# Pooling and gated delta layers: joint products of 512 columns, pooling sums by shifted additions, four PSUM banks a block

## Chip, cores and metric

The kernel runs on one core of one Trainium2 chip. The metric is the device time of one execution in microseconds (us); lower is better.

## What is computed

Two blocks of a network over 256 tokens of 2048 channels, all in float32, one after the other: a retention layer, a pooling layer, and then a block of several branches, one of them a gated delta rule. The change touches the pooling layer and the projections and the convolution of the delta rule:

```python
# pooling layer: h is the normalized input, windows 2, 4, 8, 16, one per group of 1024 channels
p = h @ w_in;  u, z = jnp.split(p, [POOL_WIDTH], axis=-1)      # 4096 channels each
win_sum = cs[:, 1:, gi] - jnp.take(cs[:, :, gi], lo, axis=1)   # cs: running sum of u over the tokens
pooled.append(win_sum / cnt)                                   # cnt = min(t + 1, w)
...
mix = (pooled - uf)
mix = jnp.einsum('bsgc,gcd->bsgd', mix, w_grp) + b_grp
return (mix.reshape(B, S, POOL_WIDTH) * scale * silu(z)) @ w_out

# delta branch: q, k, v of 2048 channels each, 16 heads of 128, z_a their output gate
qkv, z_a, ... = jnp.split(rmsnorm(x, g_pre) @ w_in, ...)
qkv = silu(causal_depthwise_conv(qkv, w_conv_qkv))             # 4 taps along the tokens
q, k, v = jnp.split(qkv, 3, axis=-1);  q, k = l2norm(q), l2norm(k)
A = einsum('bhnid,bhnjd->bhnij', k * beta, k) * decay * strict # strictly lower triangular
T = triangular_solve(eye + A, eye)
u, w = T @ (v * beta), T @ (k * beta * exp(gc))                # then a scan over chunks of 64 tokens
o_a = rmsnorm(scan(...)) * silu(z_a);  y_a = o_a @ w_br_a
```

## The kernel before

**The weight stream.** All weights come as 900 chunks of 512 KB, each two k-tiles of 128 rows by 512 columns, through a ring of four slots. For each chunk, SP issues the load into `raw` (once VectorE has split the slot's last one: semaphore `lo_done`), ScalarE rounds it to `whi` (`split_hi`, L626, once TensorE has finished the slot's last products: semaphore `multiplied`), VectorE subtracts for the rest, `wlo` (`split_lo`, L1078), and TensorE multiplies. The activations stand likewise split, as `aH` and `aL`, turned so that channels lie on the partitions. A product in full precision is the sum of three: high by high, high by low, low by high. Each engine's program is written out in order, so a helper that waits holds all behind it on that engine. A step `j` below is the chunk that TensorE is at; the splits of that step are of chunk `j + 4`.

**Two forms of a chunk.** `chunk_a` (L1930 to L1932) takes the activations as the stationary operand and gives tokens on the partitions: 12 products 512 wide. `chunk_b` (L1955, L1957, L1958) takes the weights as the stationary operand and gives channels on the partitions, 24 products 256 wide:

```python
mm(half(bank, c), whi[:, s, k, w], aH[:, kt + k], ...)
mm(half(bank, c), whi[:, s, k, w], aL[:, kt + k], ...)
ins = mm(half(bank, c), wlo[:, s, k, w], aH[:, kt + k], ...)
```

**Pooling stage** (from about 792 us, `group` on PE, ACT and DVE). Four groups, one per window, of 40 chunks: two blocks of 8 chunks give `u`, two give `z`, and 8 more chunks are the group's product with `w_grp`. All are `chunk_a`. `u` is scaled by its rows' root mean square, split into `pUH` and `pUL`, and at step 19 TensorE multiplies it with a 0/1 matrix (`pMH`) less the window's size on the diagonal: 32 products of 256 or 128 columns into banks 4 to 7. ScalarE and VectorE split those into `mH` and `mL` (L640 onwards), the stationary operand of the last 8 chunks.

**Delta stage** (from 1367 us, `delta` and `delta_late`). Four groups of four heads and 32 chunks: blocks k, q and v in `chunk_b`, with two PSUM banks each (0 and 1, 2 and 3, by turns), and the gate z in `chunk_a`. After each of the first three, ScalarE writes the convolution's last tap from PSUM (`conv_first`) and VectorE adds the other three taps from PSUM, one per step (`conv`, L1497, semaphore `conv_tap`). In step 13 VectorE forms `aT`, the eight matrices A of the group (L1574). The inverse of its 32 x 32 diagonal blocks is GpSimd's (`inverse`, 62 operations): SP takes the blocks out by DMA at step 15 (`diag_in`), back at step 16, and after the inverse out and in again at LV - 5 and LV - 4 (`diag_out`, to `iU`). LV is 34, so such steps fall into the next group's steps 0 and later. VectorE turns `iU` to `iT` (L1429, step LV - 2) and from step LV on TensorE fills in the blocks below the diagonal (`below`, first product on `iT` at L2112) and runs the scan, with VectorE's and ScalarE's steps of `delta_late` in between, down to the product of `oD` with the gate at LV + 12 (L1467) and its turning at LV + 16 to LV + 20. So between steps 13 and 34 VectorE has splits, the convolution's taps, `oD` of the group before, decays and turnings in one queue, ahead of `iT`.

Of the kernel before, what the change touches and what calls it, by code (L numbers as in the profile page):

```python
# [11 lines left out]

# [4 lines left out]
F32 = mybir.dt.float32  # L17
# [64 lines left out]
WARM = 16  # L82
NORM1_AT = {0: 2, 1: 3, 4: 4, 5: 5, 6: 6, 7: 7}
# [18 lines left out]
C_END = C_WIN + GROUPS * NT  # L102
# [7 lines left out]
def build(nc, dram):  # L110
    with ExitStack() as outer:
# [19 lines left out]
        aH = sb(outer, "aH", [P, 16, SEQ], F32R)  # L131
        aL = sb(outer, "aL", [P, 16, SEQ], F32R)
# [17 lines left out]
        with ExitStack() as s:  # L150
# [20 lines left out]
            with ExitStack() as r:  # L171
# [3 lines left out]
                pUH = sb(r, "pUH", [P, NT, GDIM], F32R)  # L175
                pUL = sb(r, "pUL", [P, NT, GDIM], F32R)
# [5 lines left out]
                pM = sb(r, "pM", [P, 3 * P])  # L182
                pMH = sb(r, "pMH", [P, 3 * P], F32R)
# [7 lines left out]
        with ExitStack() as s:  # L191
            oaH = sb(s, "oaH", [P, 16, SEQ], F32R)
            oaL = sb(s, "oaL", [P, 16, SEQ], F32R)
            with ExitStack() as r:
# [50 lines left out]
                eE = sb(r, "eE", [P, E_REAL, NT, NB])  # L245
# [35 lines left out]

        cum_rows = nc.dram_tensor("cum_rows", [NT, DN_HEADS, P], F32).ap()
# [27 lines left out]
        pu_sb, pu_lo, pz_sb, mix_ps, mix_hi, mix_lo, pm_in, pb_in, mz_add, mz_sb, pb_used = (  # L310
            sem(n) for n in "pu_sb pu_lo pz_sb mix_ps mix_hi mix_lo pm_in pb_in mz_add mz_sb pb_used".split())
# [6 lines left out]
            sem(n) for n in "dn_in conv0_sb conv_tap kqv_sb dt_sub dt_sb sq_sb sqn_sb en_sb gk_sb".split())  # L318
        scratch_out, dt_in, xn_in, u_in = (sem(n) for n in "scratch_out dt_in xn_in u_in".split())
# [44 lines left out]
        def half(bank, c):  # L364

            return PS[:, bank + c // 2, (c % 2) * SEQ:(c % 2 + 1) * SEQ]

# [21 lines left out]
        def _(sp):  # L389
# [54 lines left out]
            def delta_dma(i, first):  # L444
                q = i * (D_PER // RING) + (D_AT // RING + 2)
                for j in range(D_PER):
# [11 lines left out]
                    if j == 15:  # L458
# [5 lines left out]
                    if j == 16:  # L464
# [4 lines left out]
                    if j == LV - 5:  # L469
# [4 lines left out]
                    if j == LV - 4:  # L474
# [26 lines left out]
        def _(pool):  # L501
# [19 lines left out]
            pool.dma_start(pM[:], dram["pm"][0]).then_inc(pm_in, 16)  # L521
            row_scale(M_N2)

            def bias(i):

                pool.wait_ge(mix_hi, i * 4 + 4)
# [3 lines left out]
            with pool.Fori(1, P_N) as i:  # L530

                pool.wait_ge(pb_used, i)
                pool.dma_start(pM[:], dram["pm"][i]).then_inc(pm_in, 16)
# [47 lines left out]
            pool.wait_ge(const_set, 3)  # L581
# [37 lines left out]
        def _(act):  # L619
# [107 lines left out]
            def group(i, first):  # L727
                q = i * (P_PER // RING) + P_AT // RING
                for j in range(P_PER):
                    split_hi(q, j + RING)  # L730
                    if first and j == 1:
                        t_split_hi(T_N2 + 3, aH, 12, lambda c: C_PN + 12 + c)
                    if not first and j in (8, 16):
                        group_tail(i - 1, j // 8 - 1)
                    if j in (7, 15):
                        done(act, q, j)
                        b = j // 8
                        act.wait_ge(row_rstd, M_N2 + 1)
# [1749 lines left out]
```

## Time and profile before

| what | us |
|---|---|
| three runs: lowest, median, highest | 2625.94, 2626.36, 2626.94 |
| span of the profiled execution | 2624.1 |
| pooling stage, one group, as in the profile's windows | 112.53 |
| delta stage, one group | 108.20 |

The profiled execution is one of its own; its span runs from its first instruction to its last. The median of the three runs lies 2.3 us above that span, which is what lies around it. The windows of the profile give the busy time of each engine in a stretch; the timeline gives each instruction's start and length in us with, in brackets, how long its engine had been idle before it and what ended that idle time. Lengths of products on TensorE overlap, so only the distance of their starts, or the time of a whole chunk, is a price.

### The profile page before, as it was taken

The numbers are of one execution on the slowest core, as the hardware profiler recorded it, in microseconds if no ns is written. First come the engines' busy times: TensorE is split into PE (matmuls) and PEld (weight loads), VectorE is DVE, ScalarE is ACT, GpSimd is POOL, SyncE is SP. The second block draws the span as 40 slices with busy tenths as digits, with TensorE's granted clock in tenths as the row PEclk, the third lists the DMA queues.
The fourth block names the chain that finished last, engine by engine and source line by source line (L and its number), as shares of the span: only waits on it lengthen the run. The fifth ranks groups of instructions, "written<-read, shape, count | busy, mean of one in ns | idle before, by whom it ended". The sixth has DMA issues, their size and how long they took to land.

```text
span 2624.1 us, 36684 instructions
## 1 busy us (share of the span) xinstructions
PE 2608.1 (99%) x13284; PEld 2218.9 (85%) x13284; DVE 1960.0 (75%) x2764; ACT 1321.0 (50%) x1683; POOL 168.0 (6%) x329
## 2 busy tenths in 40 slices
PE   9999999999999999999999999999999999999998
PEld 7888888888888888888889999998888888788887
DVE  5888877776755766757457786977798999989565
ACT  5444444444444544444456454454666666564453
POOL 0000000000000000000000341413000000000000
PEclk9999999999999999999999999999999999999999
DMA  8555555555655555556655555655555655655754
GB/s 309 179 187 177 179 185 185 184 191 190 198 193 192 195 196 192 196 185 217 196 189 176 173 165 159 194 159 175 176 197 191 197 192 187 200 188 194 247 175 159
DMA packets 151674, 499.69 MB, mean 190 GB/s; under 512 B 28736, under 2 KB 29472, under 8 KB 151008
## 3 DMA queue, kind: packets, MB, share of 16 engines
q1 hardware_dynamic: 148736, 486.18, 56.0%
q0 software_dynamic: 2784, 11.40, 1.4%
q8 instruction: 104, 1.70, 0.3%
q14 instruction: 50, 0.41, 0.0%
HBM read 493.30 MB, written 4.21 MB: 190 GB/s over the span
## 4 chain that ended last, share of the span: by engine, by line
PE 97%; DVE 2%; ACT 1%; issue 0%; DMA 0%; POOL 0%; SPq 0%; DVEq 0%; ACTq 0%
PE PS L1930 27%; PE PS L1932 27%; PE PS L1931 27%; PE PS L1955 4%; PE PS L1957 4%; PE PS L1958 4%; PE PS L2096 2%; DVE yl L1624 1%; DVE wlo L1078 0%; PE PS L2103 0%; PE PS L1966 0%; PE PS L2112 0%; DVE yl L1615 0%; PE PS L2010 0%; PE PS L2020 0%
## 5 line engine op out<-in xcount | busy, mean ns | idle before, releaser
L1078 DVE TENSOR_TENSOR wlo<-raw,whi 128x1024 fp32r<-128x1024 f32 x899 | 1096.9, 1225 | 595.8 <-ACT whi L626 591.1
L626 ACT CAST whi<-raw 128x1024 fp32r<-128x1024 f32 x899 | 939.6, 1049 | 1180.7 <-PE PS L1932 1009.4
L1930 PE MATMUL PS<-whi,aH 128*128 128x512 f32 x2160 | 844.1, 391 | 3.2 <-DVE wlo L1137 1.9
L1931 PE MATMUL PS<-wlo,aH 128*128 128x512 f32 x2160 | 840.6, 389 | 0.0
L1932 PE MATMUL PS<-whi,aL 128*128 128x512 f32 x2160 | 840.6, 389 | 0.0
L1930 PEld LDWEIGHTS PS<-whi,aH 128*128 128x128 f32 x2160 | 405.6, 188 | 88.1 <-issue 2.3
L1932 PEld LDWEIGHTS PS<-whi,aL 128*128 128x128 f32 x2160 | 405.5, 188 | 84.6
L1931 PEld LDWEIGHTS PS<-wlo,aH 128*128 128x128 f32 x2160 | 405.6, 188 | 82.9
L1955 PE MATMUL PS<-aH,whi 128*128 128x256 f32 x768 | 220.8, 288 | 1.5 <-DVE aL L1114 1.5
L1957 PE MATMUL PS<-aL,whi 128*128 128x256 f32 x768 | 217.1, 283 | 0.0
L1958 PE MATMUL PS<-aH,wlo 128*128 128x256 f32 x768 | 217.1, 283 | 0.0
L1932 PE MATMUL PS<-whi,oL 128*128 128x512 f32 x512 | 199.2, 389 | 0.0
L1930 PE MATMUL PS<-whi,oH 128*128 128x512 f32 x512 | 199.2, 389 | 0.0
L1931 PE MATMUL PS<-wlo,oH 128*128 128x512 f32 x512 | 199.2, 389 | 0.0
L1955 PEld LDWEIGHTS PS<-aH,whi 128*128 128x128 f32 x768 | 147.0, 191 | 2.5 <-issue 1.7
L1957 PEld LDWEIGHTS PS<-aL,whi 128*128 128x128 f32 x768 | 147.2, 192 | 0.1
L1958 PEld LDWEIGHTS PS<-aH,wlo 128*128 128x128 f32 x768 | 147.0, 191 | 0.0
L1624 DVE SCALAR_TENSOR_TENSOR yl<-up,wl,yl 128x256 f32<-128x256 f32 x272 | 113.3, 478 | 0.2
L1931 PEld LDWEIGHTS PS<-wlo,oH 128*128 128x128 f32 x512 | 96.1, 188 | 20.1
L1932 PEld LDWEIGHTS PS<-whi,oL 128*128 128x128 f32 x512 | 96.1, 188 | 20.1
L1930 PEld LDWEIGHTS PS<-whi,oH 128*128 128x128 f32 x512 | 96.1, 188 | 19.6
L1930 PE MATMUL PS<-whi,oaH 128*128 128x512 f32 x256 | 99.9, 390 | 0.0
(357 smaller groups left out, 2570.6 us busy)
## 6 DMA issues: line engine op xcount, KB each, us to landing
raw<-in_stream SPq DMA_DIRECT2D x900, 512.0 KB, 3.3
xT<-in_xT SPq DMA_DIRECT2D x4, 512.0 KB, 7.6
H<-in_x SPq DMA_DIRECT2D x4, 512.0 KB, 10.0
pB<-in_pool_b POOLq DMA_DIRECT2D x4, 512.0 KB, 4.5
iT<-diag_in SPq DMA_DIRECT2D x16, 128.0 KB, 3.7
bg<-in_b_gate POOLq DMA_DIRECT2D x8, 256.0 KB, 3.8
out<-eb SPq DMA_DIRECT2D x8, 256.0 KB, 2.2
dmask<-in_dmask SPq DMA_DIRECT2D x4, 384.0 KB, 5.8
```

The costliest lines, as they stand in the source:

```text
L626: nc.scalar.copy(whi[:, s], raw[:, s]).then_inc(hi_done, 1 + blank)
L1078: nc.vector.tensor_tensor(wlo[:, s], raw[:, s], whi[:, s].bitcast(F32), ALU.subtract).then_inc(lo_done, 1 + blank)
L1624: nc.vector.scalar_tensor_tensor(out=to, in0=up[:, c, k:k + SEQ], scalar=w, in1=yl[:, c], op0=ALU.mult, op1=ALU.add).then_inc(long_tap[c], 1)
L1930: mm(out, hi[:, kt + k, tok], whi[:, s, k], start=kt + k == 0, stop=False)
L1931: mm(out, hi[:, kt + k, tok], wlo[:, s, k], start=False, stop=False)
L1932: ins = mm(out, lo[:, kt + k, tok], whi[:, s, k], start=False, stop=last and k == KPC - 1)
L1955: mm(half(bank, c), whi[:, s, k, w], aH[:, kt + k], start=kt + k == 0 and c % 2 == 0, stop=False, skip_group_check=True)
L1957: mm(half(bank, c), whi[:, s, k, w], aL[:, kt + k], start=False, stop=False, skip_group_check=True)
L1958: ins = mm(half(bank, c), wlo[:, s, k, w], aH[:, kt + k], start=False, stop=end, skip_group_check=True)
L2096: ins = mm(PS[rows, bank + n, h * P + at:h * P + at + width], lhsT(t, h), rhs(t, h), start=h == 0, stop=True, skip_group_check=True)
```

## The change

**Wide products.** `aH` and `aL` now lie side by side in one array `aHL`, so one product takes both: 512 columns, of which the low half of the result (high by high) lies in the first 256 columns of a PSUM bank and the other (high by low) in the last 256. The product with `wlo` is added to the first half, 256 wide. So a chunk of this form has 8 products 512 wide and 8 products 256 wide, and each 128 channels take a whole bank, four banks a block. The two halves are added later: ScalarE copies one from PSUM, and VectorE adds the other from PSUM. In the delta stage blocks k, q and v all use banks 0 to 3 and z 4 and 5; the new `chunk_b` waits per bank until it is emptied, and orders its first and last chunk by banks. The convolution reads the sum, `xc`, from SBUF.

**Pooling.** The two `u` blocks have the new form (`chunk_w`), so `u` now stands with channels on the partitions and tokens along the row. The products with the 0/1 matrix go; VectorE scales (`rrow`, a row of factors that GpSimd's queue brings through a DRAM array), adds `u` to itself shifted by 1, 2, 4 and 8 as the window needs (`window_sum`, with zeros in a margin of `PAD` columns), and combines with the window's size, in the steps of `SUM_AT`. Banks change places, and so do TensorE's waits.

**Order in the delta stage.** The splits around the last chunk of a block stand behind the additions, the `oD` product two and its last turn two steps later, `ke` two steps later, the decays at step 10. SP takes the diagonal blocks out at steps 13 and 14, not 15 and 16, and the inverse at LV - 6 and LV - 5.

```diff
+ADD_AT = (9, 17)
+SUM_AT = ((11, 13, 15, 18, 19, 20), (21, 23, 24, 25, 26, 27))
+SPLIT_AT = (22, 29)
+EVICT_AT = tuple(b * K16 + K16 - 1 for b in range(3))
...
-        aH = sb(outer, "aH", [P, 16, SEQ], F32R)
-        aL = sb(outer, "aL", [P, 16, SEQ], F32R)
+        aHL = sb(outer, "aHL", [P, 16, 2, SEQ], F32R)
+        aH, aL = aHL[:, :, 0], aHL[:, :, 1]
...
@@ SP, delta stage
-                    if j == 15:
+                    if j == 13:
                         sp.wait_ge(a_sb, i + 1)
...
-                    if j == 16:
+                    if j == 14:
                         sp.wait_ge(scratch_out, i * 128 + 80)
...
-                    if j == LV - 5:
+                    if j == LV - 6:
                         sp.wait_ge(inv_done, i + 1)
...
-                    if j == LV - 4:
+                    if j == LV - 5:
...
@@ ScalarE, group and delta
+                        nc.scalar.copy(pU[:, b, :, PAD:], wide(b)[:, :, SEQ:]).then_inc(pu_lo, 1)
...
+            def low_half(i, y, q, j):
+                n = 3 * i + y
...
+                for c in range(HG):
+                    if c < HG - 1:
+                        act.wait_ge(qkv_ps, n * 3 + c + 1)
+                    else:
+                        done(act, q, j)
+                    nc.scalar.copy(xc[:, c], PS[:, c, SEQ:]).then_inc(conv0_sb, 1)
...
+                    if j in EVICT_AT:
+                        low_half(i, EVICT_AT.index(j), q, j)
                     split_hi(q, j + RING)
...
-                    if j == (11 if first else 8):
+                    if j == 11:
                         act.wait_ge(dt_sub, i + 1)
...
@@ VectorE, group
+                        if j == ADD_AT[b]:
+                            dve.wait_ge(pu_lo, i * 2 + (b + 1))
+                            u = pU[:, b, :, PAD:]
+                            nc.vector.tensor_tensor(u, wide(b)[:, :, 0:SEQ], u, ALU.add).then_inc(pu_sb, 1)
+                        if j in SUM_AT[b][:i + 3]:
+                            window_sum(i, b, SUM_AT[b].index(j))
...
@@ VectorE, delta
-                if n == LV + 12:
+                if n == (LV + 14 if i < D_N - 1 else LV + 12):
                     dve.wait_ge(ors_sb, i + 1)
...
-                if i < D_N - 1 and n in (LV + 16, LV + 17, LV + 18, LV + 20):
+                if i < D_N - 1 and n in (LV + 16, LV + 17, LV + 18, LV + 22):
...
+            def both_halves(i, y):
+                for c in range(HG):
+                    dve.wait_ge(conv0_sb, (3 * i + y) * 8 + c + 1)
+                    nc.vector.tensor_tensor(xc[:, c], PS[:, c, 0:SEQ], xc[:, c], ALU.add).then_inc(conv_tap, 1)
...
-                    split_lo(q, j + RING)
+                    if j in EVICT_AT:
+                        both_halves(i, EVICT_AT.index(j))
+                        split_lo(q, j - 1 + RING)
+                    if j + 1 not in EVICT_AT:
+                        split_lo(q, j + RING)
...
-                    if j == 14:
+                    if j == 16:
                         dve.wait_ge(ke_sb, i * 2 + 1)
...
@@ TensorE
+            def chunk_b(q, j, kt, n, last):
...
+                by_column = last or kt == 0
+                for a, b in product(range(QT if by_column else KPC), range(KPC if by_column else QT)):
+                    c, k = (a, b) if by_column else (b, a)
+                    if kt + k == 0 and n is not None:
+                        pe.wait_ge(conv_tap, (n - 1) * 16 + c + 1)
+                    w = slice(c * P, (c + 1) * P)
+                    mm(PS[:, c], whi[:, s, k, w], aHL[:, kt + k].rearrange("p a n -> p (a n)"), start=kt + k == 0, stop=False,
+                       skip_group_check=True)
+                    ins = mm(PS[:, c, 0:SEQ], wlo[:, s, k, w], aH[:, kt + k], start=False, stop=last and k == KPC - 1,
+                             skip_group_check=True)
+                    if last and k == KPC - 1 and c < QT - 1:
+                        ins.then_inc(qkv_ps, 1)
...
-                pe.wait_ge(mix_lo, i * 4 + 4)
                 for w in range(2):
-                    pe.wait_ge(pz_sb, i * 2 + (w + 1))
                     for k in range(4):
+                        if not w and k % 2 == 0:
+                            pe.wait_ge(mix_lo, i * 2 + (k // 2 + 1))
```

Two places in the engines' order follow, each before and after. A row is a line, an operation, its result and operands, its size, and in brackets the semaphores that it waits for. The first is VectorE in the delta stage, group 1, from step 13 on. `raw` to `wlo` is a chunk's split, `aT` are the matrices A, `oD` the product with the gate for group 0, `ke` the scaled keys, `yD` the convolution's taps. Before:

```order
L1078 TENSOR_TENSOR wlo<-raw,whi 128x1024 [waits hi_done]
L1570 TENSOR_TENSOR ed<-en,dT 128x4 [waits en_sb,dt_sb]
L1574 SCALAR_TENSOR_TENSOR aT<-PS,en,dT 128x128 [waits a_ps]
L1574 SCALAR_TENSOR_TENSOR aT<-PS,en,dT 128x128 x7
L1078 TENSOR_TENSOR wlo<-raw,whi 128x1024 [waits hi_done]
L1467 SCALAR_TENSOR_TENSOR oD<-oD,oms,zD 128x128 [waits zd_sb,ors_sb]
L1467 SCALAR_TENSOR_TENSOR oD<-oD,oms,zD 128x128 x7
L1581 TENSOR_SCALAR ke<-PS,ed 128x128 [waits ke_sb]
L1581 TENSOR_SCALAR ke<-PS,ed 128x128 x3
L1078 TENSOR_TENSOR wlo<-raw,whi 128x1024 [waits hi_done]
L1497 SCALAR_TENSOR_TENSOR yD<-PS,wcv,yD 128x255 [waits conv0_sb,multiplied]
L1497 SCALAR_TENSOR_TENSOR yD<-PS,wcv,yD 128x255 [waits conv0_sb] x3
```

After:

```order
L1123 TENSOR_TENSOR wlo<-raw,whi 128x1024 [waits hi_done]
L1643 TENSOR_TENSOR ed<-en,dT 128x4 [waits en_sb,dt_sb]
L1647 SCALAR_TENSOR_TENSOR aT<-PS,en,dT 128x128 [waits a_ps]
L1647 SCALAR_TENSOR_TENSOR aT<-PS,en,dT 128x128 x7
L1572 TENSOR_TENSOR xc<-PS,xc 128x256 [waits conv0_sb] x4
L1123 TENSOR_TENSOR wlo<-raw,whi 128x1024 [waits hi_done] x2
L1565 SCALAR_TENSOR_TENSOR yD<-xc,wcv,yD 128x255 [waits conv0_sb] x4
L1123 TENSOR_TENSOR wlo<-raw,whi 128x1024 [waits hi_done]
L1535 SCALAR_TENSOR_TENSOR oD<-oD,oms,zD 128x128 [waits zd_sb,ors_sb]
L1535 SCALAR_TENSOR_TENSOR oD<-oD,oms,zD 128x128 x7
L1654 TENSOR_SCALAR ke<-PS,ed 128x128 [waits ke_sb]
L1654 TENSOR_SCALAR ke<-PS,ed 128x128 x3
```

The four additions to `xc` now stand right behind `aT`, ahead of two splits that stood before and after the `oD` product; `oD` and `ke` come behind them.

The second is TensorE at the change from block q to block v (the second to the third) in the same group, the last products of one chunk and the first of the next. Before:

```order
L1958 MATMUL PS<-aH,wlo 128x256
L1955 MATMUL PS<-aH,whi 128x256 [waits lo_done,conv_tap]
L1957 MATMUL PS<-aL,whi 128x256
L1958 MATMUL PS<-aH,wlo 128x256
L1955 MATMUL PS<-aH,whi 128x256
```

After:

```order
L2032 MATMUL PS<-aHL,wlo 128x256
L2030 MATMUL PS<-aHL,whi 128x512 [waits conv_tap,lo_done]
L2032 MATMUL PS<-aHL,wlo 128x256
L2030 MATMUL PS<-aHL,whi 128x512
L2032 MATMUL PS<-aHL,wlo 128x256
L2030 MATMUL PS<-aHL,whi 128x512 [waits conv_tap]
L2032 MATMUL PS<-aHL,wlo 128x256
```

Before, the first product waits for a bank emptied a block earlier; now each bank's first product waits for the additions on the block just finished.

## Rows read from the trace of the kernel before

**Rows 1.** Page: span, busy engines, chain that ended last.

```profile
span 2624.1 us, 36684 instructions
...
PE 2608.1 (99%) x13284; PEld 2218.9 (85%) x13284; DVE 1960.0 (75%) x2764; ACT 1321.0 (50%) x1683; POOL 168.0 (6%) x329
...
PE 97%; DVE 2%; ACT 1%; issue 0%; DMA 0%; POOL 0%; SPq 0%; DVEq 0%; ACTq 0%
```

**Rows 2.** Windows: length, busy PE, PEld, DVE, ACT, POOL, clock; pooling, delta, within delta.

```profile
1017.61:1130.14 112.53, 112.53 (x514) 93.83 (x513) 75.92 (x95) 52.44 (x61) 1.07 (x2) 1.00 0.59 194
1482.30:1590.50 108.20, 108.20 (x884) 103.69 (x884) 87.02 (x165) 55.08 (x70) 33.95 (x66) 1.00 0.54 168
...
1531.40:1588.50 57.10, 57.10 (x395) 53.34 (x393) 55.55 (x107) 28.97 (x36) 29.77 (x63) 1.00 0.60 184
```

**Rows 3.** Timeline of ACT: start, length; splits in pooling, then in delta.

```profile
1083.06 1.05 ACT L626 CAST whi<-raw 128x1024 fp32r<-128x1024 f32 x1 [1.67 <-PE PS L1932]
1085.78 1.05 ACT L626 CAST whi<-raw 128x1024 fp32r<-128x1024 f32 x1 [1.67 <-PE PS L1932]
...
1534.45 1.05 ACT L626 CAST whi<-raw 128x1024 fp32r<-128x1024 f32 x1 [1.83 <-PE PS L1958]
1537.33 1.05 ACT L626 CAST whi<-raw 128x1024 fp32r<-128x1024 f32 x1 [0.36 <-PE PS L1958]
```

**Rows 4.** Timeline of TensorE, delta stage: start, length, two neighbouring products.

```profile
1531.31 0.28 PE L1955 MATMUL PS<-aH,whi 128*128 128x256 f32 x1
1531.43 0.28 PE L1957 MATMUL PS<-aL,whi 128*128 128x256 f32 x1
```

**Rows 5.** Chain: start, length; first products that read `iT`, groups 0 to 3.

```profile
1482.30 1.02 PE PS L2112 x32
...
1590.46 1.02 PE PS L2112 x32
...
1698.61 1.02 PE PS L2112 x32
...
1806.29 1.08 PE PS L2112 x32
```

**Rows 6.** Timeline of DVE: `iT` of group 0, stretch of group 1, `iT` again.

```profile
1479.68 1.25 DVE L1429 STREAM_TRANSPOSE iT<-iU 128x1024 f32<-128x1024 f32 x1 [0.73 <-DMA iU<-diag_out]
...
1530.99 2.15 DVE L1574 SCALAR_TENSOR_TENSOR aT<-PS,en,dT 128x128 f32<-128x128 f32 x8
1533.06 1.22 DVE L1078 TENSOR_TENSOR wlo<-raw,whi 128x1024 fp32r<-128x1024 f32 x1
...
1586.42 1.23 DVE L1078 TENSOR_TENSOR wlo<-raw,whi 128x1024 fp32r<-128x1024 f32 x1
1588.51 1.25 DVE L1429 STREAM_TRANSPOSE iT<-iU 128x1024 f32<-128x1024 f32 x1 [0.86 <-DMA iU<-diag_out]
...
1697.04 1.25 DVE L1429 STREAM_TRANSPOSE iT<-iU 128x1024 f32<-128x1024 f32 x1 [0.97 <-DMA iU<-diag_out]
...
1804.98 1.25 DVE L1429 STREAM_TRANSPOSE iT<-iU 128x1024 f32<-128x1024 f32 x1 [0.75 <-DMA iU<-diag_out]
```

**Rows 7.** Groups by shape: busy, mean ns; four subtractions on the timeline.

```profile
L640 ACT CAST aH<-PS 128x256 fp32r<-128x256 f32 x16 | 4.8, 387 | 5.4 <-PE PS L1966 5.4
L1401 DVE TENSOR_TENSOR sg<-PS,bg 128x1024 f32<-128x1024 f32 x8 | 9.8, 1221 | 0.1
...
2440.98 1.41 DVE L1112 TENSOR_TENSOR oaL<-PS,oaH 128x256 fp32r<-128x256 f32 x4
```

**Rows 8.** Timeline of DVE in the pooling stage, one split.

```profile
1056.94 1.23 DVE L1078 TENSOR_TENSOR wlo<-raw,whi 128x1024 fp32r<-128x1024 f32 x1 [1.49 <-ACT whi L626]
```

**Rows 9.** Timeline of the DMA queue SP, delta group 1.

```profile
1539.14 1.85 SPq L462 DMA_DIRECT2D diag_in<-aT  x4
...
1581.14 2.55 SPq L473 DMA_DIRECT2D diag_out<-xi  x4
```

**Rows 10.** Timeline of DVE while GpSimd inverts, delta group 3.

```profile
1778.19 1.38 DVE L1078 TENSOR_TENSOR wlo<-raw,whi 128x1024 fp32r<-128x1024 f32 x1
```

More of the change, by code:

```diff
@@ L11 @@
 from contextlib import ExitStack
+from itertools import product
 import concourse.bass as bass
@@ L366, in half, with wide, steps_before @@
             return PS[:, bank + c // 2, (c % 2) * SEQ:(c % 2 + 1) * SEQ]
+        def wide(b):
+            return PS[:, 4 - 4 * b:8 - 4 * b]
+        def steps_before(i, b):
+            return sum(2 * (g + 5) for g in range(i)) + b * (i + 5)
         def heads(bank):
@@ L751, in group @@
                         b = j // 8 - 2
[L752 removed]
+                        if first and b == 0:
+                            act.wait_ge(row_rstd, M_N2 + 1)
+                        by_token(pZ[:, :, b * NB:(b + 1) * NB], 4 + 2 * b, ACT.Silu, M_N2, pz_sb)
             def group_tail(i, w):
@@ L1545, in delta @@
                         delta_late(i - 1, j + D_PER)
[L1546 removed]
+                    if first and j == 7:
+                        bias_decays()
+                        for k in range(1, TAPS):
+                            conv(i, 0, k)
+                        decays()
+                    if not first and 7 <= j <= 9:
+                        conv(i, 0, j - 6)
+                    if not first and j == 10:
                         dve.wait_ge(dt_in, i * (16 * NT))
                         log_decays(i, dT)
[L1549 to L1560 removed]
                     if first and j == 14:
@@ L1952, in chunk_b @@
                     for c in range(QT):
-                        w = slice(c * P, (c + 1) * P)
-                        end = last and k == KPC - 1
-                        mm(half(bank, c), whi[:, s, k, w], aH[:, kt + k], start=kt + k == 0 and c % 2 == 0, stop=False,
+                        w, out = slice(c * P, (c + 1) * P), wide(b)[:, c]
+                        mm(out, whi[:, s, k, w], aHL[:, kt + k].rearrange("p a n -> p (a n)"), start=kt + k == 0, stop=False,
                            skip_group_check=True)
-                        mm(half(bank, c), whi[:, s, k, w], aL[:, kt + k], start=False, stop=False, skip_group_check=True)
-                        ins = mm(half(bank, c), wlo[:, s, k, w], aH[:, kt + k], start=False, stop=end,
+                        ins = mm(out[:, 0:SEQ], wlo[:, s, k, w], aH[:, kt + k], start=False, stop=last and k == KPC - 1,
                                  skip_group_check=True)
@@ L2163, in delta @@
                     b = j // K16
-                    if j == 0 and not first:
-                        pe.wait_ge(conv_tap, i * 36)
-                    if j == K16 and not first:
-                        pe.wait_ge(zd_sb, i)
-                    if j == 2 * K16 or j == 3 * K16:
-                        pe.wait_ge(conv_tap, i * 36 + 12 * (b - 1))
+                    if j == 3 * K16:
+                        pe.wait_ge(sq_sb, i * 2 + 2)
+                    if first and j == 1:
+                        pe.wait_ge(ee_sb, 2)
                     if first and j in (1, 3, 5):
```

209 lines of the change are left out of this document (114 added, 95 removed).

## The prediction

> **What bounds the kernel now.** I read the page first: TensorE is busy for 99% of 2624.1 us and carries 97% of the chain that ended last [rows 1]. So a shorter TensorE stream pays in full, as long as no other engine becomes late. Next the windows: a pooling group takes 112.53 us and a delta group 108.20, TensorE busy throughout at the full 2.4 GHz (granted clock 1.00), VectorE 75.92 and 87.02 [rows 2]. These averages mislead: inside a delta group, from 1531.4 to 1588.5, VectorE is busy 55.55 of 57.10 us [rows 2]. Its timeline there is one unbroken queue from the split at 1533.06, right behind the `aT` operations, to the split at 1586.42 (19 splits with other work between them), then 0.86 us of waiting for a DMA, then the transpose of `iT` [rows 6]. TensorE's first product on `iT` follows: at 1482.30, 1590.46, 1698.61 and 1806.29 for the four groups [rows 5], against `iT` done at 1480.93, 1589.76, 1698.29 and 1806.23 (start plus 1.25) [rows 6]. The margin is 1.37, 0.70, 0.32 and 0.06 us. So TensorE sets the pace in both stages, and in the delta stage VectorE is just in time, three groups out of four.
>
> The price of a product comes from the splits that TensorE releases: one per chunk, 2.72 us apart in pooling and 2.88 in delta [rows 3]. 12 products of 512 columns in 2.72 us is 0.2267 each; 24 products of 256 in 2.88 is 0.1200, as the starts 1531.31 and 1531.43 show [rows 4]. The lengths in the timeline (0.28) overlap and are no price. At 2.4 GHz the columns alone take 0.2133 and 0.1067, so each product has a fixed 13.3 ns, whatever its width.
>
> **Part 1, wide products in delta.** Per pair of k-tile and 128-column block, three 256-column products become one of 512 and one of 256. A chunk of 8 pairs costs 8 x (0.2267 + 0.1200) = 2.773 us against 2.88, 0.107 less. Three blocks of 8 chunks in 4 groups: 96 x 0.107 = **-10.2 us**, all on TensorE's path. The alternation of widths is not in the trace; its bounds are 0 (a wide product as dear as two narrow ones) and twice the 13.3 ns, from which I take the fixed part as the two neighbouring widths give it. The Trainium skill ("TensorE: Matmul & The Clock Gate", Back-to-back issue gap) gives about 2.5 ns beside the columns; by it 768 pairs would save 1.9 us. The rows here show five times that, at two widths alike, so the trace does not agree with it.
>
> **Part 2, pooling.** The sums on TensorE go: 112.53 - 40 x 2.72 = 3.73 us per group, -14.9 in all. Two of the four projection blocks change from 12 products of 512 to 8 of 512 and 8 of 256: 2.773 against 2.72, 16 chunks a group, 64 x 0.053 = +3.4. Together **-11.5 us**. VectorE takes the sums over: per half group an addition from PSUM, a scaling, one to four shifted additions, a last combination, each 1024 wide, 1.22 us by the nearest row [rows 7]. They stand one to a step from step 17 to 29, each beside a split: 1.23 [rows 8] + 1.22 = 2.45 us of a 2.72 us chunk; today the queue idles 1.49 us per step there [rows 8]. TensorE reads the result at chunks 32 and 34, and the last split of it stands at step 29, so I cost it at nothing; the four-dimensional operands have no row, and at twice the price the longest group would fall behind 0.9 us a step over 12 steps, 10 us, of which some 5 is covered by the ring of four chunks: +5 at most. ScalarE has fewer operations than now.
>
> **Part 3, four banks a block.** With 512 columns per 128 channels a block fills banks 0 to 3, so the next block must wait until its bank is emptied: ScalarE copies the low half (0.387 us, nearest row) and VectorE adds the other half (0.42) [rows 7]. This happens 8 times with TensorE waiting (blocks 0 to 1 and 1 to 2), the third block's successor uses banks 4 and 5. Take block 1 to 2 of group 1. Chunk 15 begins at 1531.31 and by the new column order finishes a bank every 0.693 us. ScalarE learns of a finished chunk 0.26 us late (1531.31 + 2.88 = 1534.19, and its split starts at 1534.45 [rows 3]). It is held by a 1.05 us split to 1532.6, and copies the banks then and at 1533.0, 1533.65 and 1534.34. VectorE comes free from `aT` at 1533.06, so bank 0 is added by 1533.5; chunk 16 wants it at 1534.08, and each further bank 0.693 later, which the additions keep ahead of (the last at 1535.2 against 1536.2). TensorE waits for none: cost 0, upper bound 0.6 us each, 5 in all, if VectorE were a microsecond later.
>
> **Part 4, what these additions do to VectorE's queue.** Here I expect the gain of Part 1 to go. All of it stands in the saturated stretch. The four additions of step 15 finish at 1535.2 instead of releasing VectorE at 1533.06: 2.1 us, mostly waiting for TensorE's last column, with the splits of chunks 18 and 19 queued behind. The four at step 23 find their data ready: 1.41 us [rows 7]. The rest of the queue is the same work in another order (the `od` product and the last turn of `oD` a few steps later, the decay logarithms from step 6 to 10, where there was idle time). So `iT` is 3.5 us later in VectorE's own time, less the DMA wait, which goes. TensorE comes sooner: 12 chunks x 0.107 = 1.28 us (9 chunks in the last group, 0.96). Wait before the first product on `iT`: group 1, 3.5 + 1.28 - 0.70 - 0.86 = 3.2; group 2, 3.5 + 1.28 - 0.32 - 0.97 = 3.5; group 3, 3.5 + 0.96 - 0.06 - 0.75 = 3.65. Group 0 has no tail of an earlier group in its queue and idles in between; its 1.37 + 0.73 is enough, 0. Sum **+10.4 us**. A split that is late earlier in the stretch makes TensorE wait there and by as much less at `iT`.
>
> **Part 5, the transfers sooner.** On SP the four reads of `aT` issue at 1539.14 today, though `aT` is ready at 1533.1 [rows 6, 9]; two steps earlier they start about 6 us sooner, and GpSimd's inverse with them. Behind them SP holds the loads of chunks 22 and 23 for some 3 us. A load goes out when a slot's split is done and has some four chunks, 11 us, until the next split of that slot must be; I cost 3 us of that at nothing, and at 3 us a group if VectorE's lag had used it up. At the other end the write at 1581.14 [rows 9] moves a step up, but behind a chunk load that waits for VectorE's split, which is now late: it goes out at about the same time and lands before VectorE reaches `iT`. Value: the DMA waits of 0.73 to 0.97 [rows 6], counted in Part 4.
>
> **The sum.** -10.2 - 11.5 + 10.4 = -11.3 us. The profiled execution spans 2624.1; the runs' median is 2626.36, 2.3 us more around the span, which the change leaves alone. 2626.4 - 11.3 = **2615 us**.
>
> **Rivals.**
> A, no wait at `iT`: VectorE is not as late as I work out, because the additions at step 15 overlap idle time or the earlier transfers matter more. For it: the reordering moves work out of that stretch's front. Against: the unbroken queue. Time: 2626.4 - 21.7 = 2605; half the wait, 2610.
> B, the wide products do not do what they say: the fixed 13.3 ns stays with the columns. Delta gains nothing, pooling -14.9 + 64 x 0.16 = -4.7, and the wait at `iT` is 3.5 less 1.56, 1.29 and 0.81, 7.0: 2628.7. Against: two widths give one fixed part. With the 2.5 ns of the Trainium skill ("TensorE: Matmul & The Clock Gate", Back-to-back issue gap) in place of 0 it would be -14.3 - 1.9 + 7.7, 2618; the rows do not bear that out either.
> C, slower: VectorE's two-input operations and GpSimd's inverse take turns. One split lasts 1.38 instead of 1.22 beside the inverse [rows 10]. If each of the stretch's 19 splits and 8 additions lost 0.16, `iT` would be 4.3 us later in three groups: 2615 + 13 = 2628. From 7.2 us of wait per group the change loses. Against: the inverse already runs beside this stretch today, 29.77 us of it [rows 2].
>
> **How the numbers follow.** Forecast 55% (its own range 2611 to 2619, an error of 1.2 us per group), A 22%, B 10%, C 8%, 5% unexplained. The range reaches down to A and up to the forecast with 5 us of Part 2 or 3: 2604 to 2622. 0.2% is 5.3 us, about what a measurement of this kernel can tell from no change: faster means under 2621.1. That is the forecast, A and a small part of B: 0.79. Within: 0.14. Slower by more than that: 0.07.
>
> **What would show it.** Right: wide chunks 2.77 us apart; no PSUM sums; pooling groups of 109.7 us with no TensorE wait; TensorE idle about 3.4 us before the first product on `iT` in groups 1 to 3, released by VectorE and not by a DMA, and none in group 0; delta groups 1 and 2 about as long as now. Wrong: chunks of 2.88; TensorE waiting on `conv_tap` at block changes; `iT` released by DMA; a wait for `mix_lo`.

## The result

The changed kernel takes 2643.18 us (median of five runs, 2638.93 to 2643.82) against 2626.36 us before: 0.6% slower, ratio 1.0062 with a 95% interval of 1.0049 to 1.0074. The forecast was 2615.0, faster. The profiled execution of the changed kernel spans 2642.2 us, 18.1 more than the 2624.1 of [rows 1]; the readings below account for these 18.1.

The page of the changed kernel, span, busy engines and the shares of the chain that ended last:

```profile
span 2642.2 us, 35514 instructions
...
PE 2618.0 (99%) x12644; PEld 2183.3 (83%) x12644; DVE 2018.6 (76%) x2848; ACT 1333.7 (50%) x1711; POOL 169.9 (6%) x332
...
PE 97%; DVE 2%; issue 1%; ACT 0%; DMA 0%; SPq 0%; POOL 0%; DVEq 0%; ACTq 0%
```

TensorE has 640 products fewer and is busy 9.9 us longer, which no removed work explains. In the chain, "issue" has come up from 0 to 1%. The chain of the changed kernel (start, length, what; "issue" is a wait that the profile gives to nothing) shows it at the place the prediction named, ahead of the first products on `iT` (now L2201) in groups 0 to 3; these rows answer to [rows 5]:

```profile
1480.45 1.02 PE PS L2201 x32
...
1587.02 3.06 issue
1590.07 1.56 PE PS L2201 x32
...
1699.79 2.90 issue
...
1812.17 3.12 issue
```

None in group 0, then 3.06, 2.90 and 3.12 us. But look at what comes behind: the 32 small products last 1.56 us instead of 1.02. The windows around the first of the waits (length, busy PE, granted clock, DMA share, GB/s) say why:

```profile
1587.00:1590.00 3.00, 0.02 (x1) 1.00 0.78 258
1590.00:1594.00 4.00, 3.93 (x39) 0.53 0.80 245
1594.00:1598.00 4.00, 4.00 (x42) 0.61 0.75 246
1598.00:1602.00 4.00, 4.00 (x36) 1.00 0.40 135
```

Behind the wait TensorE runs for some 7 us at about half speed, the 1.2 GHz level, and the windows behind the other two are alike. Busy time times (1 - clock) is 3.4 us for each of the three (here 3.93 x 0.47 + 4.00 x 0.39), 10.3 in all, on top of the 9.1 of waiting.

The rest is elsewhere, and can be seen by setting ScalarE's splits of the two kernels side by side, chunk by chunk. In the stage that writes the retention layer's output, which the change does not touch, the timeline of ScalarE has, before:

```profile
600.43 1.05 ACT L626 CAST whi<-raw 128x1024 fp32r<-128x1024 f32 x1 [1.67 <-PE PS L1932]
603.15 1.05 ACT L626 CAST whi<-raw 128x1024 fp32r<-128x1024 f32 x1 [1.67 <-PE PS L1932]
```

and in the changed kernel:

```profile
598.67 1.05 ACT L656 CAST whi<-raw 128x1024 fp32r<-128x1024 f32 x1 [1.73 <-PE PS L2005]
601.46 1.05 ACT L656 CAST whi<-raw 128x1024 fp32r<-128x1024 f32 x1 [1.74 <-PE PS L2005]
```

A chunk of the same 12 products takes 2.79 us where it took 2.72: by the starts of the products, 0.2324 us each instead of 0.2267, 5.7 ns more, at the same granted clock. It is so for every product whose stationary operand is `oH`, `oL`, `mH`, `mL`, `oaH`, `oaL`, `ubH` or `ubL` (3072 products, in 256 chunks that take 17.2 us more; the expectations below reckon with a first reading of 5.5 ns and 16.9 us), and for none of those on `aHL` in the same form. By stage the chunks drift apart by +4.4 us in the retention output, -9.1 in pooling, +4.4 in the pooling output, +12.5 in the delta stage and +6.1 behind it, in the stages on `oaH` and `ubH`.

One pooling group and one delta group as windows (length, busy PE, PEld, DVE, ACT, POOL, clock, DMA share, GB/s), to be read against [rows 2]:

```profile
953.89:1064.14 110.25, 110.25 (x546) 92.94 (x545) 86.84 (x105) 51.41 (x56) 0.68 (x2) 1.00 0.58 196
...
1592.00:1704.60 112.60, 109.70 (x689) 95.39 (x689) 92.35 (x180) 59.34 (x83) 34.60 (x66) 0.97 0.51 164
```

A pooling group is 2.28 us shorter than before, a delta group with its wait and the slow clock 4.4 longer.

### The profile page after: what moved, and what is told of

Its sections match the earlier page's. It is cut to its first block, busy times and chain, and to the rows that moved or that the text cites. A ratio compares the mean times of both kernels' runs of the same rounds, so it can differ in the third digit from the quotient of the medians.

```text
span 2642.2 us, 35514 instructions
## 1 busy us (share of the span) xinstructions
PE 2618.0 (99%) x12644; PEld 2183.3 (83%) x12644; DVE 2018.6 (76%) x2848; ACT 1333.7 (50%) x1711; POOL 169.9 (6%) x332
## 4 chain that ended last, share of the span: by engine, by line
PE 97%; DVE 2%; issue 1%; ACT 0%; DMA 0%; SPq 0%; POOL 0%; DVEq 0%; ACTq 0%
PE PS L2003 25%; PE PS L2004 25%; PE PS L2005 25%; PE PS L2030 7%; PE PS L2046 4%; PE PS L2032 3%; PE PS L2048 2%; PE PS L2185 2%; DVE yl L1697 1%; DVE wlo L1123 0%; PE PS L2192 0%; PE PS L2201 0%; PE PS L2056 0%; DVE yl L1688 0%; PE PS L2100 0%
## 5 line engine op out<-in xcount | busy, mean ns | idle before, releaser
L2003 PE MATMUL PS<-whi,aHL 128*128 128x512 f32 x1904 | 745.2, 391 | 2.6 <-DVE wlo L1123 1.4
L2005 PE MATMUL PS<-whi,aHL 128*128 128x512 f32 x1904 | 742.1, 390 | 0.0
L2004 PE MATMUL PS<-wlo,aHL 128*128 128x512 f32 x1904 | 741.8, 390 | 0.0
L2003 PEld LDWEIGHTS PS<-whi,aHL 128*128 128x128 f32 x1904 | 358.0, 188 | 78.1 <-DVE wlo L1123 2.0
L2005 PEld LDWEIGHTS PS<-whi,aHL 128*128 128x128 f32 x1904 | 357.9, 188 | 74.9
L2004 PEld LDWEIGHTS PS<-wlo,aHL 128*128 128x128 f32 x1904 | 358.1, 188 | 73.0
L2030 PE MATMUL PS<-aHL,whi 128*128 128x512 f32 x768 | 280.2, 406 | 1.6 <-DVE aHL L1159 1.6
L2032 PE MATMUL PS<-aHL,wlo 128*128 128x256 f32 x768 | 217.5, 283 | 0.0
L2046 PE MATMUL PS<-aHL,whi 128*128 128x512 f32 x512 | 177.8, 394 | 0.0
L2030 PEld LDWEIGHTS PS<-aHL,whi 128*128 128x128 f32 x768 | 146.4, 191 | 36.7 <-issue 2.0
L2032 PEld LDWEIGHTS PS<-aHL,wlo 128*128 128x128 f32 x768 | 147.4, 192 | 0.0
L2048 PE MATMUL PS<-aHL,wlo 128*128 128x256 f32 x512 | 141.8, 277 | 0.0
L2046 PEld LDWEIGHTS PS<-aHL,whi 128*128 128x128 f32 x512 | 96.0, 187 | 22.3
```

Of the source, the lines that this page charges most:

```text
L2003: mm(out, hi[:, kt + k, tok], whi[:, s, k], start=kt + k == 0, stop=False)
L2004: mm(out, hi[:, kt + k, tok], wlo[:, s, k], start=False, stop=False)
L2005: ins = mm(out, lo[:, kt + k, tok], whi[:, s, k], start=False, stop=last and k == KPC - 1)
L2030: mm(PS[:, c], whi[:, s, k, w], aHL[:, kt + k].rearrange("p a n -> p (a n)"), start=kt + k == 0, stop=False, skip_group_check=True)
L2032: ins = mm(PS[:, c, 0:SEQ], wlo[:, s, k, w], aH[:, kt + k], start=False, stop=last and k == KPC - 1, skip_group_check=True)
L2046: mm(out, whi[:, s, k, w], aHL[:, kt + k].rearrange("p a n -> p (a n)"), start=kt + k == 0, stop=False, skip_group_check=True)
```

## Experiments

Four things need a cause: the products that became dearer without being touched, the wait at `iT`, the clock behind it, and the price of the wide products. Chunks of the new form are 2.77 us apart in the changed kernel's pooling stage and 2.83 in most of its delta stage, where they hold no other products:

```profile
852.00 1.05 ACT L656 CAST whi<-raw 128x1024 fp32r<-128x1024 f32 x1 [1.73 <-PE PS L2048]
854.78 1.06 ACT L656 CAST whi<-raw 128x1024 fp32r<-128x1024 f32 x1 [1.72 <-PE PS L2048]
...
1638.60 1.05 ACT L656 CAST whi<-raw 128x1024 fp32r<-128x1024 f32 x1 [2.03 <-PE PS L2032]
1641.43 1.05 ACT L656 CAST whi<-raw 128x1024 fp32r<-128x1024 f32 x1 [1.78 <-PE PS L2032]
```

Each experiment stands against runs of the kernel before that were taken beside it, so that kernel's median varies, from 2626.4 to 2627.1.

### Placement

The table `cols` grew by 32 columns of four bytes (`C_NSZ`), so that every tensor declared behind it moved by 128 bytes against the weights `whi` and `wlo` and against `aHL`, which stand ahead of it. Theory P (placement): that is where the dearer products come from. Theory S (schedule): it is the order of the work, that is, what else runs or where the products stand in the program.

e1 moves the tensors by another 128 bytes in the changed kernel, which makes 256 in all. To make room, `eE` is laid over `kqv`:

```diff
         cols = sb(outer, "cols", [P, C_END])
+        spare = sb(outer, "spare", [P, 32])
...
-                with ExitStack() as b:
-                    eE = sb(b, "eE", [P, E_REAL, NT, NB])
+                eE = kqv[:, 0:2].rearrange("p a (t x) n -> p a t (x n)", t=NT)
```

> The changed kernel with 128 bytes left free behind the table of columns (and eE laid over kqv, to make room), so that every tensor behind the table stands at the same place within 256 bytes as in the kernel before. Theory P (placement): a product whose stationary operand was moved by 128 bytes costs 5.5 ns more (0.2322 against 0.2267 us); 3072 such products in the changed kernel (oH, oaH, mH, ubH and their low parts) make 16.9 us; with them back the chunks on oH are 2.72 us apart again, and the time is 2643.2 - 16.9 = 2626. Theory S (schedule: the products are slower because of what else runs, or of where they stand in the program): the chunks on oH stay at 2.79 and the time at 2643. In both the wait of about 3 us before the first product on iT stays in groups 1 to 3.

Measured: 2628.23 us against 2626.62, ratio 1.0004 (0.9995 to 1.0014). Chunks on `oH` are at 2.72 again. The waits stay:

```profile
1579.21 3.06 issue
...
1690.39 2.90 issue
...
1802.60 3.13 issue
```

So 15.0 of the 16.8 us by which the changed kernel lost go with this edit. It has two parts, the placement and `eE`; e2 has the first alone.

e2 moves the same tensors of the kernel before by 128 bytes, and does nothing else:

```diff
         cols = sb(outer, "cols", [P, C_END])
+        spare = sb(outer, "spare", [P, 32])
```

> The kernel before with 128 bytes left free behind the table of columns, nothing else. Theory P: chunks on oH, oaH, mH, ubH at 2.79 us instead of 2.72, time 2626.4 + 16.9 = 2643. Theory S: no change, 2626.

Measured: 2644.53 us against 2626.62, ratio 1.0066 (1.0049 to 1.0083): 17.9 us for 128 unused bytes, with chunks on `oH` at 2.79. For these products Theory S is out.

e3 puts the same 128 bytes ahead of everything:

```diff
+        spare = sb(outer, "spare", [P, 32])
         raw = sb(outer, "raw", [P, RING, KPC, NB])
```

> The kernel before with 128 bytes left free ahead of the very first tensor, so that all tensors move alike, the streamed operands whi and wlo too. If what counts is how the two operands of a product stand to each other (theory P, relative), nothing changes: 2626. If it is the place of the stationary operand by itself (theory P, absolute), all 900 chunks take 0.066 us more: some 2680. Theory S: 2626.

Measured: 2626.75 us in one run, no change, and chunks on `oH` at 2.72. So it is not the place of an operand by itself, but how operands stand to one another.

e4 moves by 64 bytes instead of 128:

```diff
         cols = sb(outer, "cols", [P, C_END])
+        spare = sb(outer, "spare", [P, 16])
```

> The kernel before with 64 bytes left free behind the table of columns instead of 128. Theory P: if the place within 128 bytes counts too, chunks on oH are slower than 2.72 here as well; if only 128-byte halves count, 2.72 or 2.79 according to the half that each 64 bytes fall in. Theory S: 2626 and 2.72.

Measured: 2649.63 us in one run, 23 more; chunks on `oH` 2.80 us apart, against 2.79 at 128 bytes. 256 chunks of 0.08 us more are 20.5 of these; the rest was not followed up:

```profile
599.78 1.05 ACT L627 CAST whi<-raw 128x1024 fp32r<-128x1024 f32 x1 [1.75 <-PE PS L1933]
602.58 1.05 ACT L627 CAST whi<-raw 128x1024 fp32r<-128x1024 f32 x1 [1.75 <-PE PS L1933]
```

Shifts of 0 and 256 bytes (e1) are good, 64 and 128 are not. Other distances were not tried.

### The wait at `iT` and the clock

e5 gives TensorE two more chunks before it needs `iT`, on the basis of e1:

```diff
-LV = 34
+LV = 36
...
-                    if j == LV - 6:
+                    if j == 28:
...
-                    if j == LV - 5:
+                    if j == 29:
...
-                if n == LV - 2:
+                if n == 32:
```

> As e1, and TensorE's first product on iT with all that follows it two chunks later (LV 36), while the transfers and VectorE's transpose to iT keep their steps (28, 29, 32). So TensorE has 5.5 us of other work where it waited 3.06, 2.90 and 3.13 us in e1. In e1 the granted clock behind those waits was 0.5 to 0.9 for 4 to 9 us, which by length times (1 - clock) is 1.7, 3.4 and 1.7 us. Theory wait and clock: both go, 9.1 + 6.8 = 15.9, time 2628.2 - 15.9 = 2612. Theory wait alone (what the slow clock costs is made up elsewhere): 2619. Rival: VectorE is the bound of these groups and the wait comes back at a later step of the chain: 2628.

Measured: 2626.58 us against 2626.58 of the kernel before, ratio 0.9997 (0.9988 to 1.0007). The waits at `iT` are gone and others stand in their place. What TensorE waits for (us in total, times, longest):

```profile
PE PS L2192 <- DVE oD L1522: 7.1, 3, 2.4
...
PE PS L2030 <- DVE xc L1572: 2.2, 3, 0.8
```

The chain shows how the first comes about:

```profile
1510.66 0.48 ACT vn L876
...
1511.16 1.28 ACT L942
...
1512.45 0.79 ACT dT L942
...
1513.42 1.04 ACT whi L656
...
1515.62 0.70 DVE oD L1522
```

Two chunks later, the chain from `iT` to `oD` falls into step 11, where ScalarE now has a table load and the exponential of the decays in its queue. The rival was half right: the wait came back at a later step, though behind ScalarE's queue and not VectorE's. The clock fell behind these waits too; the window behind the first (length, busy PE, clock, DMA share, GB/s):

```profile
1516.45:1521.00 4.55, 4.55 (x25) 0.62 0.34 119
```

Busy time times (1 - clock) is 1.7 us here and as much behind the other two. So e5 has waits of 9.3 us and a slow clock, as e1 has, and gains nothing. e6 takes one chunk instead of two, `LV = 35`, with the rest as in e5.

> As e5 with one chunk instead of two (LV 35): 2.77 us of other work against waits of 2.9 to 3.1, so 0.1 to 0.4 us of each wait stay. If the clock falls only behind a long wait, it stays at 1.00 here and the time is that of e5 plus 1; if any wait at this place brings it down, some 5 us more than e5.

Measured: 2616.29 us in one run. TensorE's waits from 1470 to 1830 us:

```profile
PE PS L2003 <- DVE wlo L1123: 2.6, 4, 1.0
PE PS L2030 <- DVE wlo L1123: 1.9, 2, 0.9
PE PS L2201 <- issue: 0.4, 1, 0.4
```

and the clock in the stretches around the first product on `iT`, group 1:

```profile
1564.00:1576.00 12.00, 10.55 (x51) 1.00 0.51 148
1576.00:1584.00 8.00, 7.92 (x73) 1.00 0.80 234
1584.00:1592.00 8.00, 8.00 (x82) 1.00 0.79 216
```

VectorE is still short: TensorE waits 4.9 us in all, now for splits of chunks, in pieces of up to 1 us. But the clock stays at 1.00. The prices of the chunks are nearly as in e1 (mostly 2.83 in pooling, a stage 0.7 us shorter than in e1, and mostly 2.77 in delta). From e1 to e6, waits fall by 4.2 us (9.1 to 4.9), and the 6.8 that the slow clock cost in e1 are gone; that makes 11.0, against 10.4 between the profiled executions (2625.1 and 2614.7) and 11.9 between the times. So the larger part is the clock. This is one run; e10 below, with the same `LV`, took 2613.5 to 2616.4 in four. A wait in one piece of 3 us costs more than the same wait in pieces here.

e9 is e1 (`LV` at 34) and takes 1.12 us from VectorE's queue:

```diff
@@ VectorE
-                    if j == 16:
-                        dve.wait_ge(ke_sb, i * 2 + 1)
-                        for h in range(HG):
-                            ins = nc.vector.tensor_scalar(ke[:, h], heads(6)[:, 0, h], ed[:, h:h + 1], None, ALU.mult)
-                        ins.then_inc(ke_sb, 1)
@@ ScalarE
+                    if j == 14:
+                        act.wait_ge(a_ps, i + 1)
+                        act.wait_ge(ke_sb, i * 2 + 1)
+                        for h in range(HG):
+                            ins = nc.scalar.activation(ke[:, h], heads(6)[:, 0, h], ACT.Copy, scale=ed[:, h:h + 1])
+                        ins.then_inc(ke_sb, 1)
```

> As e1 (LV 34), with the scaling of the keys (ke, four operations, 1.12 us) on ScalarE at step 14 instead of VectorE at step 16. If VectorE's unbroken queue sets when iT is ready, the waits of 3.06, 2.90 and 3.13 us at the first product on iT become about 2.0, and the time falls by 3.3 and by a part of the 6.8 that the slow clock behind them costs: 2619 to 2625. If the transfers of the inverse set it, the waits stay and the time is 2628.

Measured: 2623.0 us in one run, within what was expected. The waits are 1.83, 1.79 and 2.14:

```profile
1579.78 1.83 issue
...
1690.08 1.79 issue
...
1798.54 2.14 issue
```

So work taken from VectorE comes off the wait one for one: its queue sets `iT`, not the transfers. The clock (same columns as above) differs from wait to wait, 1.00 behind the shortest and 0.51 behind the longest:

```profile
1691.88:1697.00 5.12, 5.12 (x81) 1.00 0.85 280
1581.60:1585.00 3.40, 3.40 (x39) 0.62 0.73 224
1800.68:1807.00 6.32, 6.32 (x43) 0.51 0.69 220
```

### The price of the wide products

e7 is e5 with narrow products in the delta stage:

```diff
-                    mm(PS[:, c], whi[:, s, k, w], aHL[:, kt + k].rearrange("p a n -> p (a n)"), start=kt + k == 0, stop=False,
-                       skip_group_check=True)
+                    mm(PS[:, c, 0:SEQ], whi[:, s, k, w], aH[:, kt + k], start=kt + k == 0, stop=False,
+                       skip_group_check=True)
+                    mm(PS[:, c, SEQ:], whi[:, s, k, w], aL[:, kt + k], start=False, stop=False,
+                       skip_group_check=True)
```

> As e5, but each 512-column product of blocks k, q and v is two products of 256 columns again (same banks, additions and order); the pooling stage keeps its wide products. This prices the wide products of the delta stage by themselves, with no wait on iT. By the prediction's prices a chunk takes 2.88 instead of 2.773, 96 x 0.107 = 10.2 us more than e5; if the wide products stand at 2.83 as in most of the changed kernel's delta stage, 96 x 0.05 = 4.8.

Measured: 2632.14 us, against e5's 2626.58: 5.6 us for 96 chunks. That is no clean price, since the clock differs too. Behind the waits for `oD`, 2.27 us each, it fell at one of three places in e7, where in e5 (2.38 us each) it fell at all three; the second place in e7:

```profile
1628.80:1634.00 5.20, 5.11 (x45) 1.00 0.40 126
```

The profiled executions, with a mean clock of 0.998 in e7 and 0.996 in e5, are only 0.3 us apart (2627.7 and 2627.4). So the price has to be read from the chunks. Those of the delta stage that hold no other products are 2.88 apart in e7, the prediction's price of narrow products. In e5 those of groups 1 and 2 are mostly at 2.83, those of groups 0 and 3 at 2.77.

So a pair of a wide and a narrow product has two prices. By the starts of TensorE's products, the two together have 64 cycles of 2.4 GHz beside their columns in one state and about 80 in the other; most of the difference lies with the wide one, 40 to 45 cycles against some 55. The state holds for many chunks. The changed kernel has the cheap state in pooling and the dear one in most of the delta stage, e1 the other way round: its pooling chunks are 2.83 apart.

```profile
851.18 1.05 ACT L656 CAST whi<-raw 128x1024 fp32r<-128x1024 f32 x1 [1.78 <-PE PS L2048]
854.01 1.05 ACT L656 CAST whi<-raw 128x1024 fp32r<-128x1024 f32 x1 [1.78 <-PE PS L2048]
```

e8 is e5 with the products in another order, two wide ones and then two narrow ones. The pooling blocks' part of the edit is shown; chunks 1 to 6 of each delta block have the same order:

```diff
...
-                for k in range(KPC):
-                    for c in range(QT):
+                for k, pair in product(range(KPC), ((0, 1), (2, 3))):
+                    for c in pair:
                         w, out = slice(c * P, (c + 1) * P), wide(b)[:, c]
                         mm(out, whi[:, s, k, w], aHL[:, kt + k].rearrange("p a n -> p (a n)"), start=kt + k == 0, stop=False,
                            skip_group_check=True)
+                    for c in pair:
+                        w, out = slice(c * P, (c + 1) * P), wide(b)[:, c]
                         ins = mm(out[:, 0:SEQ], wlo[:, s, k, w], aH[:, kt + k], start=False, stop=last and k == KPC - 1,
                                  skip_group_check=True)
```

> As e5, with another order of the same products in the pooling blocks and in chunks 1 to 6 of each delta block: two of 512 columns, then two of 256. In e1 the 64 wide pooling chunks took 2.83 us and most delta chunks 2.77, in the changed kernel 2.77 and 2.83. If the dearer state (16 cycles of 2.4 GHz per pair) comes with a change of width, half the changes leave at most half of it: at least 1.7 us less than e5 in pooling. If it does not hang on the order, no change, within 1 us.

Measured: 2623.67 us, against 2626.58 of e5: 2.9 less, with the wide pooling chunks at 2.785, all but the first of the stage:

```profile
850.80 1.05 ACT L656 CAST whi<-raw 128x1024 fp32r<-128x1024 f32 x1 [1.74 <-PE PS L2060]
853.59 1.05 ACT L656 CAST whi<-raw 128x1024 fp32r<-128x1024 f32 x1 [1.73 <-PE PS L2060]
```

By the starts of the products the pooling stage is 2.0 us shorter than in e5; the clock, 0.998 in the profiled execution against 0.996, has a part in the rest. In e8, e10 and e11, which all have this order, no such pooling chunk stands at 2.83 or at 2.77, so the price hangs on the order of widths. What puts an alternating sequence into one state or the other is not settled.

### What was learned, put together

e10 is e6 with the order of e8, e11 is e10 with the keys on ScalarE as in e9.

> e6 (one chunk later, LV 35) with the order of e8 (two wide products, then two narrow). e6 took 2616.3 in one run; e8's pooling chunks took 2.785 where e5's took 2.83, 64 x 0.045 = 2.9 less; in the delta stage e6 stood at 2.77, where the pairs give 2.785, 72 x 0.015 = 1.1 more. Sum 2614.5. If e6's time was a chance, near 2626.

> e10 with the keys scaled on ScalarE as in e9. In e6 TensorE still waited some 4 us in all for VectorE's splits in the stretch ahead of iT; 1.12 us less in VectorE's queue per group takes 1 us off in three groups: 2611.5. If what binds there is something else, as e10.

Measured: e10 2615.06 us, ratio 0.9956 (0.9939 to 0.9972) to the kernel before; e11 2612.50 us, ratio 0.9944 (0.9927 to 0.9961). e11 is faster than both kernels of this case, by 14.6 us than the 2627.09 of the kernel before that were measured beside it. Both times lie within 1 us of what was expected. TensorE in e11 still waits 2.7 us from 1470 to 1830 us, against 9.1 in e1, at a clock of 1.00 throughout.

## Why the prediction was wrong

**What bounds the kernel, and the place of the loss: right.** TensorE sets the pace, VectorE's queue between `aT` and `iT` is the only other bound. The first product on `iT` waits in groups 1 to 3 and not in group 0, by 3.06, 2.90 and 3.12 us where 3.2, 3.5 and 3.65 were worked out, 9.1 in all against 10.4. VectorE's timeline in group 1 runs from 1532.34 to `iT` without a gap that is shown, and no DMA releases it; `iT` ends at 1589.97 and the product on it starts at 1590.07 (to be read against [rows 6]):

```profile
1532.00 0.42 DVE L1572 TENSOR_TENSOR xc<-PS,xc 128x256 f32<-128x256 f32 x1 [0.28 <-ACT xc L895]
1532.34 2.35 DVE L1123 TENSOR_TENSOR wlo<-raw,whi 128x1024 fp32r<-128x1024 f32 x2
...
1587.59 1.23 DVE L1123 TENSOR_TENSOR wlo<-raw,whi 128x1024 fp32r<-128x1024 f32 x1
1588.73 1.24 DVE L1497 STREAM_TRANSPOSE iT<-iU 128x1024 f32<-128x1024 f32 x1
```

The additions of step 15 end at 1532.4, 2.0 us behind the `aT` operations (2.1 was the estimate); those of step 23 take 1.40 (1.41). e9 shows that this queue is the cause.

**Part 4, the step that failed first: a wait was priced at its length alone.** "Sum +10.4 us" takes the wait at `iT` for its whole cost. TensorE idle in one piece of 3 us then ran at half its clock for some 7 us, 10.3 us more in the three groups, so that a delta group is 4.4 us longer, not about as long as before. [Rows 2] only showed a clock of 1.00, in groups without such a wait, and the prediction did not bound what happens to the clock if there is one. The Trainium skill ("TensorE: Matmul & The Clock Gate", What's actually happening) says that the throttled clock is the default and that activity releases it; the windows above, half speed behind the wait and full speed again after some microseconds of products, agree.

**What no part costed: the 32 columns.** The constants of the change were read and counted at nothing. They move every tensor behind the table by 128 bytes, which makes 3072 products 5.7 ns dearer, 17.2 us. This is the largest term that was left out, and without it the changed kernel would have been within 2 us of the kernel before (e1). It touches stages that the change does not, so no sum over the edits could find it; a look at where the tensors lie would have shown that they move, though no row of the trace of before shows the price of that.

**Part 1: the price of alternating widths.** "-10.2 us" rests on two fixed shares of 13.3 ns, measured where neighbours have the same width. That is what the cheap state shows (2.77 per chunk). In the dear state a chunk takes 2.83, and 96 of them would save 4.8. The bounds for this term, 0 and twice 13.3 ns, held the truth; the value was read from rows that do not alternate.

**Part 2: right in mechanism and, by itself, in size.** 110.25 us per group instead of 109.7; the difference is the 8 chunks on `mH`, 0.067 us each. The shifted additions on VectorE hide, and TensorE waits for nothing from 740 to 1360 us. Without the placement but in the dear state, e1 has 110.55: 112.53 - 3.73 + 16 x 0.11. So it was luck that the changed kernel's pooling chunks met the price of 2.773: which state they would be in was not foreseen.

**Part 3: right.** In the changed kernel TensorE does not wait for `xc` at a block change. The table of its waits has no such row; e5 has 2.2 us of them, where the chain behind `iT` lies later.

**Part 5: right.** The blocks of `aT` go out at 1530.48 instead of 1539.14, 8.7 us sooner where about 6 was expected, and the inverse's result leaves at 1578.91, behind a chunk's load that waited for VectorE:

```profile
1530.48 1.82 SPq L481 DMA_DIRECT2D diag_in<-aT  x4
...
1536.58 42.29 SPq L414 DMA_DIRECT2D raw<-in_stream  x14
1578.91 2.57 SPq L492 DMA_DIRECT2D diag_out<-xi  x4
```

The transfers ended in time, but nobody profited, since VectorE was later than they were.

**The sum, corrected.** Pooling -11.3 (-9.1 as measured, less the 2.2 that placement adds on `mH`), wide products in delta -6.8, waits +9.1, clock +10.3, placement +17.2: +18.5, against +18.1 measured between the two profiled executions. The -6.8 is four times 1.7, by the rows of the result: from the first product on `iT` of group 0 to group 1's wait the changed kernel takes 106.57 us (1480.45 to 1587.02), and before it was 108.16 to the next group's product [rows 5]. That is 1.6 less, and 1.85 and 1.6 in the next two groups when the 3.4 us of slow clock are taken off. 24 chunks at 2.83 would make 1.2 a group, which suggests that some of the chunks are in the cheap state; which ones is not resolved, because many hold other products too.

The rivals: A (no wait) and C (VectorE and GpSimd in each other's way) did not come true; C had the sign for another reason. B was half true, since the fixed share does in part stay; its three waits add up to 6.8 us, not 7.0.

## What to carry to other kernels

When an edit adds a few bytes to a table, look at what is declared behind it: the operands of every product move against each other, and stages that the edit never names can become slower; compare unchanged stages first. Price a wait of TensorE with the granted clock behind it, not by its length alone: several short waits cost less here than one long one, and equal waits did not always cost the same. And when an engine's queue without gaps feeds a consumer at a fixed step, one step more of distance may be worth more than the work saved; but follow the chain behind that step, since two steps collided with the next queue (e5).

## What the runs showed of the hardware

**Two operands' distance.** A product with a 128-column stationary operand that was moved by 128 bytes against the streamed one takes 0.2324 us instead of 0.2267 (the changed kernel, e2); by 64 bytes, 0.233 (e4, 2.80 per chunk of 12); by 256, 0.2267 (e1); moved together by 128, no change in time (e3). The Trainium skill ("TensorE: Matmul & The Clock Gate", Step-by-step: what each phase is for) says that TensorE has two independent read ports, one for the streamed operand and one for the weights, and that loading the next weights takes nothing from the running product. These runs do not show the two as independent: their distance in memory costs 2.5% at 128 bytes. Which of the loads meets which stream was not separated.

**Two states of one sequence.** 512- and 256-column products by turns ran at 2.77 or at 2.83 us per 16 in the same program (the changed kernel, e1, e5), and stayed in a state for whole blocks; two of each by turns ran at 2.785 in pooling (e8).

**The clock.** Behind waits of 2.9 to 3.1 us TensorE's clock fell to the lower level each time, and busy time times (1 - clock) came to 1.7 to 3.4 us (the changed kernel and e1). Behind three waits of 2.4 us it fell each time in e5 (0.62 to 0.69 in the windows behind them) and twice in e8 (0.67, 0.68 and 1.00); behind three of 2.27 us, once in e7 (0.70, twice 1.00). Behind waits of 1.8 to 2.1 us it was 1.00 once and 0.5 to 0.6 twice (e9). With waits of up to 1 us it stayed at 1.00 (e6, with 10.55 us of products in 12.00, and e10 and e11 from 1470 to 1830 us). So waits of the same length, in the same program, were followed by either level.
